# First modulation and block f computed tile by tile of features, with f's weights outside the ring of slots

## The reference

```
mod = einsum(silu(cond), w_ada[l]) + b_ada[l]          # (6 * 1024) per group
sh1, sc1, g1, sh2, sc2, g2 = split(mod, 6)
hn  = rmsnorm(x, norm_mix[l]) * (1.0 + sc1) + sh1
proj = einsum('bld,de->ble', hn, w_in[l])              # q,k,v of attention, retention, HGRN2
...                                                    # three mixers, w_out, gated residual, MoE
```

## Time and profile before

| | us |
|---|---|
| median of 3 runs | 951.66 |
| lowest and highest | 951.46, 954.39 |
| profiled execution: time | 953.32 |
| profiled execution: span | 951.5 |
| TensorE busy in it | 920.2 (97%) |
| VectorE busy | 431.9 (45%) |
| ScalarE busy | 158.7 (17%) |

### The profile page before, as it was taken

How to read it: one execution, slowest core, us unless ns; L and a number is a source line. 1 busy time by engine, 2 the same in 40 slices (tenths; PEclk the granted TensorE clock), 3 DMA queues, 4 the chain that set the end, 5 groups by cost and what they waited for, 6 DMA issues and landing times.

```text
span 951.5 us, 13385 instructions
## 1 busy us (share of the span) xinstructions
PE 920.2 (97%) x5191; PEld 499.6 (53%) x5197; DVE 431.9 (45%) x780; ACT 158.7 (17%) x408; POOL 63.7 (7%) x96
## 2 busy tenths in 40 slices
PE   5999999999999999999999999999999999999997
PEld 2755575568553444344437556657864444443442
DVE  1385887742423122232145999876252321222223
ACT  2212024320210100010111211432021001000100
POOL 1112230020000000000000223000000000000001
PEclk9999999999999999999999999999999999999999
DMA  9996574675999999999996632601189999999993
GB/s 365 401 390 268 222 267 177 243 278 213 408 420 422 421 421 421 421 422 420 421 421 252 225 124 91 235 32 38 35 364 422 421 421 421 421 421 421 421 421 137
DMA packets 48430, 303.63 MB, mean 319 GB/s; under 512 B 7680, under 2 KB 7696, under 8 KB 14960
## 3 DMA queue, kind: packets, MB, share of 16 engines
q1 hardware_dynamic: 42368, 291.52, 75.2%
q0 software_dynamic: 2960, 8.63, 2.6%
q10 hardware_dynamic: 3040, 2.62, 0.8%
HBM read 300.10 MB, written 2.65 MB: 318 GB/s over the span
## 4 chain that ended last, share of the span: by engine, by line
PE 84%; DVE 9%; DMA 3%; ACT 2%; issue 1%; SPq 0%; DVEq 0%; ACTq 0%
PE ps L427 82%; PE ps L461 2%; DMA ring<-in_w_in 2%; ACT eP L1582 1%; DMA ring<-in_w_ada 1%; DVE fa L1263 1%; DVE rt L1057 1%; DVE eP L1361 1%; DVE stat L1057 1%; DVE xy L1257 1%; DVE eP L1359 1%; DVE hnT L1105 0%; DVE sq L1214 0%; DVE proj L1290 0%; DVE proj L1224 0%
## 5 line engine op out<-in xcount | busy, mean ns | idle before, releaser
L427 PE MATMUL ps<-ring,proj 128*64 128x512 f32 x1024 | 226.3, 595 | 1.0 <-ACT proj L1829 1.0
L427 PE MATMUL ps<-ring,hnT 128*128 128x512 f32 (+1 forms) x576 | 203.2, 505 | 2.3 <-issue 1.2
L427 PEld LDWEIGHTS ps<-ring,hnT 128*128 128x128 f32 x576 | 106.9, 191 | 75.9 <-issue 67.7
L427 PEld LDWEIGHTS ps<-ring,proj 128*64 128x64 f32 x1024 | 72.6, 137 | 132.8 <-issue 131.1
L427 PE MATMUL ps<-hnT,ring 128*64 128x128 f32 (+2 forms) x576 | 74.0, 342 | 2.9 <-DVE hnT L1105 1.6
L427 PEld LDWEIGHTS ps<-hnT,ring 128*64 128x64 f32 (+1 forms) x576 | 60.7, 160 | 13.9 <-issue 2.9
L427 PEld LDWEIGHTS ps<-proj,xs 128*128 128x128 f32 x512 | 58.4, 192 | 12.5 <-issue 11.4
L427 PE MATMUL ps<-proj 128*128 128x512 f32 x128 | 61.7, 607 | 0.0
L427 PE MATMUL ps<-proj,xs 128*128 128x128 f32 x512 | 61.4, 278 | 0.1
L1553 DVE COPY proj<-ps 128x512 f32<-128x512 f32 x16 | 11.1, 692 | 108.0 <-PE ps L427 108.0
L427 PE MATMUL ps<-ring,silT 128*32 128x512 f32 x384 | 48.8, 630 | 9.6 <-DVE silT L1073 6.9
(11 more groups left out here) (231 smaller groups left out, 920.9 us busy)
## 6 DMA issues: line engine op xcount, KB each, us to landing
ring<-in_w_gate SPq DMA_DIRECT2D x64, 1024.0 KB, 14.4
ring<-in_w_down SPq DMA_DIRECT2D x64, 1024.0 KB, 16.8
ring<-in_w_ada SPq DMA_DIRECT2D x48, 1024.0 KB, 8.6
ring<-in_w_in SPq DMA_DIRECT2D x28, 1024.0 KB, 8.5
eP<-in_w_up SPq DMA_DIRECT2D x16, 1024.0 KB, 15.8
wT<-in_w_up SPq DMA_DIRECT2D x16, 1024.0 KB, 17.9
fa<-in_w_up SPq DMA_DIRECT2D x16, 1024.0 KB, 17.7
xy<-in_w_up SPq DMA_DIRECT2D x16, 1024.0 KB, 19.1
```

Of the source, the lines that this page charges most:

```text
L427: ins = nc.tensor.matmul(*a, **k)
```

## The change

At the start of layer 0 the adaLN product and block f go by tiles of features.

- The two sixths (0, x) of w_ada are stored a second time, as `ada_x`: eight tiles of 1 MB, each with all rows for one tile of 128 features, shift and scale. One tile alone gives the modulation of its features. TensorE makes of each eight matmuls of 256 columns into four quarters of bank 1 (`sums_of_feature`); ScalarE copies them (256 columns); two matmuls of 2 columns with the new constant `pick` add the quarters and turn them (`modulation_of_feature`); VectorE and ScalarE finish the tile k of hnT; and `feature_of_first_block` adds tile k to all four heads of f at once, in two banks (eight matmuls of 256 columns). The sums of tile k + 1 stand between the picks and the f matmuls of tile k.
- f's two halves are loaded into eP and wT (slots 8 and 9), ahead of adaLN tiles 1 and 4 (`ROWS_AHEAD`). The ring's count begins at two (`FIRST_SLOT`).
- condT, x and the first constants are loaded by SP, ahead of all weights; GpSimd keeps mods. ScalarE starts with group 0 when its x has landed.
- The zeros for TensorE are 14 matmuls, at the very start; they also clear the two banks of f.
- `ADA_BEHIND` of layer 0 goes from (2, 3, 3, 3, 3, 2, 3, 2) to (0, 0, 2, 9, 3, 2, 3, 2): the loads of b stand behind two adaLN slots. The diagonals stand behind block a's last quarter and these two steps; of the nine steps around b, three stand behind each group's first half and three behind b.
- VectorE bounds both heads' pairs first (`bounded(0)`, `bounded(1)`), then makes the gates.

Layer 1 is as before. The diff, cut:

```diff
-ADA_BEHIND = ((2, 3, 3, 3, 3, 2, 3, 2), (0, 0, 0, 0, 0, 3, 0, 0))
+ADA_BEHIND = ((0, 0, 2, 9, 3, 2, 3, 2), (0, 0, 0, 0, 0, 3, 0, 0))
+ROWS_AHEAD = (1, 4)
+FIRST_SLOT = 2
...
                 if l == 0:
-                    for step in EARLY:
-                        load_ada(*step)
+                    for k in range(KC):
+                        if k in ROWS_AHEAD:
+                            r = ROWS_AHEAD.index(k)
+                            load_rows(*IN_BLOCKS[0], r, RING + r)
+                        load(flat_slot, ap["ada_x"][k])
...
+                def sums_of_feature(k):
+                    pe.wait_ge(S("bank1_free"), c.claim(1))
+                    s = slot()
+                    for i in range(KC):
+                        q = slice(32 * (i % 4), 32 * (i % 4) + 32)
+                        last = mm(ps[q, 1, 0:2 * P], silT[:, i, :], ..., start=i < 4, stop=i >= 4)
+                    owed.append(s)
...
+                    f_banks = [next_bank() for _ in range(2)]
+                    pe.wait_ge(c.of("zero", 0), c.at("zero", 0))
+                    stream_zeros(f_banks[0], 12)
+                    stream_zeros(f_banks[1], 2)
+                    normalized_group("hn1", "xn1", 0, banks=(4, 5))
+                    sums_of_feature(0)
+                    normalized_group("hn1", "xn1", 1, banks=(6, 0))
+                    ss = []
+                    for k in range(KC):
+                        modulation_of_feature(k)
+                        if k + 1 in ROWS_AHEAD:
+                            ss.append(slot(RING + len(ss)))
+                        if k + 1 < KC:
+                            sums_of_feature(k + 1)
+                        feature_of_first_block(k, ss, f_banks)
...
                 ss = open_block("b")
+                if not l:
+                    diagonal(0)
+                    diagonal(1)
                 for g in range(NG):
                     b = by_token("b", g, 0, ss)
+                    if not l:
+                        ada_steps(3)
                     level(0, 2 * g)
...
-                ada_behind("b")
+                ada_steps(ADA_BEHIND[l][3] % 6)
                 ss = open_block("i")
...
-                gates(0)
+                bounded(0)
+                if l:
+                    gates(0)
+                    bounded(1)
+                else:
+                    bounded(1)
+                    gates(0)
                 gates(1)
```

More of the change, by code:

```diff
@@ L70, in host_constants @@
     at = [(32 * (2 * a + h), g) for h in range(2) for a in range(2) for g in range(NG)]
+    c["pick"] = np.stack([t % 32 == g for g in range(NG)], 1)
     c["pickm"] = np.stack([t == row + g for row, g in at], 1)
@@ L333, in build @@
         ADA = {"x": (0, 1), "g": (2, 5), "y": (3, 4)}
-        EARLY = [(0, "x", k) for k in range(KC)]
         LATER = [[(0, "g", k) for k in range(KC)] + [(0, "y", k) for k in range(KC)] + [(1, "x", k) for k in range(KC)],
@@ L386, in _ @@
                     for r in range(2):
[L387 to L389 removed]
+                        if l or name != "f":
+                            load_rows(name, col, n, r)
                     for step in itertools.islice(steps, behind):
@@ L482, in claim_for_norm, with normalized_group @@
                 return b
-            def normalized_group(stage, factors, g, ahead=None, first=None):
+            def normalized_group(stage, factors, g, ahead=None, banks=(None, None)):
                 xv = x[:, g].rearrange("p (k q) -> p k q", k=KC)
                 for h in range(2):
-                    b = claim_for_norm() if h or first is None else first
+                    if banks[h] is None:
+                        b = claim_for_norm()
+                    else:
+                        b = banks[h]
+                        pe.wait_ge(S(f"bank{b}_free"), c.claim(b))
                     if not h:
@@ L553, in at_change @@
                         ada_step(*step)
-                if l == 0:
-                    b = claim_for_norm()
-                    for step in EARLY[0:5]:
-                        ada_step(*step)
-                        stream_zeros(b, 3)
-                    pe.wait_ge(c.of("begin_dma"), c.at("begin_dma"))
-                    normalized_group("hn1", "xn1", 0, first=b)
-                    normalized_group("hn1", "xn1", 1)
-                    for step in EARLY[5:]:
-                        ada_step(*step)
-                    modulation_by_feature(0, 0)
-                else:
+                def sums_of_feature(k):
[3 more added lines that the diff above has]
+                        q = slice(32 * (i % 4), 32 * (i % 4) + 32)
+                        last = mm(ps[q, 1, 0:2 * P], silT[:, i, :], by_k(s, 2 * P)[:, i] if i < KH else flat_slot(s)[:, 2 * P * i:2 * P * (i + 1)], start=i < 4, stop=i >= 4)
+                        if i < KC - 1:
+                            pay(last)
+                    last.then_inc(c.fills(1, "ada", 0, "x", k), 1)
+                    owed.append(s)
@@ new lines, in modulation_of_feature @@
+                def modulation_of_feature(k):
+                    pe.wait_ge(S("bank7_free"), c.claim(7))
+                    pe.wait_ge(c.of("modX", 0, 0, k), c.at("modX", 0, 0, k))
+                    for a in range(2):
+                        last = mm(ps[:, 7, NG * a:NG * (a + 1)], modX[:, 2 * P * (k % 2) + P * a:2 * P * (k % 2) + P * (a + 1)], C["pick"], start=True, stop=True)
+                        if not a:
+                            pay(last)
+                    last.then_inc(c.fills(7, "modT", 0, 0, k), 1)
@@ new lines, in feature_of_first_block @@
+                def feature_of_first_block(k, ss, banks):
+                    for g in range(NG):
+                        pe.wait_ge(c.of(f"hn1S{g}", k), c.at(f"hn1S{g}", k))
+                    for p in range(2):
+                        for hl in range(2):
+                            for d in range(2):
+                                col = 64 * (2 * p + hl) + 256 * d
+                                last = mm(ps[64 * d:64 * d + 64, banks[p], 256 * hl:256 * (hl + 1)], by_k(ss[k // KH], 512)[:, k % KH, col:col + 64], hnT[:, k, :], start=False, stop=(k == KC - 1), skip_group_check=True)
+                                if k == KC - 1 and hl and d:
+                                    last.then_inc(c.fills(banks[p], "projP", "f", p), 1)
+                                else:
+                                    pay(last)
@@ L1969, in laid_out @@
     w_out = np.asarray(inputs["w_out"]).reshape(L, D, 2, BLK).transpose(0, 2, 1, 3)
+    first = np.asarray(inputs["w_ada"])[0, :, 0:2 * D].reshape(P, KC, 2, KC, P)
+    out["ada_x"] = first.transpose(3, 0, 1, 2, 4).reshape(KC, P, KC * 2 * P)
     out["w_out"] = halves(w_out, KH).reshape(L, 2, 2, P, KH * BLK)
```

95 lines of the change are left out of this document (53 added, 42 removed).

## The result

The changed kernel takes 962.28 us, median of four runs (960.29 to 963.24), beside 953.02 us of the kernel before on the same chip: ratio 1.0089, 95% interval 1.0063 to 1.0115. It is slower by 0.9%, more than forecast and outside the range. The profiled execution is the fastest of the four: 960.29 us, span 958.5 us, 7.0 us over the 951.5 us of before.

A forecast was written before the change was run, and what follows sets the result against it. TensorE was taken to bound the kernel (84% of the chain). Terms -7.3 (end of f), -1.2 (wait of a), +1.9 (VectorE), +7.9 (slot 1), +1.6 (clock) gave +2.9 us, forecast 954.6 us, range 950.0 to 958.5 us.

The forecast's parts named there:

- T: End of block f: forecast at 41.3 us, 7.3 us earlier than 48.60 us; upper bound 44 us.
- E: End of block b's last quarter, when its slot 1 comes free: forecast at T + 52.5 us.
- some 0.4 us later for the first slot: third at 14.4 us: Start of the weight queue: four small loads ahead on SP delay the first slot 0.4 us; third slot lands at 14.4 us.
- The round: First stage, per feature on TensorE: pick, next feature's sums, f matmuls and changes between them, taken as 3.45 us.
- VectorE: Between T and block i: TensorE waits 0.3 us for hq, 0.6 and 1.0 us for banks; sum 1.9 us, bounds 0 and 4.
- The slot of b: Ahead of i: loads queue behind b's slot 1, released only at E; i at E + 12.5 us, cost 7.9 us.
- The clock: At the start of i: idle stretches bring the clock to half, costing 1.6 us, bounds 0 and 2.5 us.
- Behind i everything is queued as before ... so I take nothing back: After block i: same queue and slots falling together again, so later steps shift by one constant; 0 us.
- slot 1: Ring slot holding part of b; kernel gets over 0.3% faster if its wait costs under 2.2 us with the clock up.
- rival 1: First stage at transfer pace, clock holds: T 38.3 to 40 us, time 950.0 to 951.7 us; chance 0.30.
- rival 2: Clock falls inside the feature loop too, 1.7 us each: 956.3 to 958 us, chance 0.12; low throughout: 973 us, 0.02.
- (3): Ahead of i: slot 1 wait doesn't reach TensorE; i at 98.4 us, -6.5 us, 945.2 us; chance 0.06.

The follow-up runs named there:

- experiment 9: Changed kernel with the small loads (condition, token tiles, constants) issued by GpSimd again, as in the kernel before: 966.7 us, one run.
- Experiment 4: Changed kernel with each feature's f matmuls one round later, behind the next feature's picks and sums: 961.91 us, ratio 1.0083 to the kernel before.
- experiment 10: Changed kernel with the first layer's gates computed ahead of the bounded form again, as in the kernel before: 963.41 us, one run.
- experiment 3: Changed kernel with block b behind five adaLN steps, six left around it: 958.52 us, ratio 1.0041 to the kernel before.
- 12: Changed kernel with b behind eight adaLN steps, seven zero matmuls in the first tile wait, eight more ScalarE copies: 955.2 us, ratio 1.0026.
- experiment 2: Changed kernel with the three waits between b and i filled with matmuls nobody reads: 959.19 us, ratio 1.0042 to the kernel before.
- experiment 7: Changed kernel with 8 more small copies on ScalarE in the first stage: 958.12 us, ratio 1.0051 to the kernel before.
- experiment 1: Changed kernel's new first stage with the old order behind f, so b lies in slots 6 and 7 again: 957.89 us, ratio 1.0049.
- 8: Changed kernel with old order behind f, f matmuls one round later, f's halves ahead of tiles 2 and 6, 8 ScalarE copies: 956.57 us, ratio 1.0029.
- 11: Changed kernel with seven more matmuls of zeros at the entry of the first layer's experts: 963.46 us, one run.
- 13: Changed first stage with old order behind f, plus seven zero matmuls ahead of the second tile's sums and eight ScalarE copies: 957.29 us, ratio 1.0036.
- experiment 5: The kernel before, unchanged, run again for a second profile: 953.67 us.

## Why the prediction was wrong

**The way to i was right in its shape, with three terms off.** Forecast 106.3 us, measured 107.34 us; that it lies so near is partly luck, since an error of +2.6 us (T) and one of -2.0 us (from T to E) cancel.

- T, the end of f: 41.3 forecast, 43.92 measured, near the upper bound of 44. The step that failed first is "some 0.4 us later for the first slot: third at 14.4 us": it came at 15.75 us. The 1.1 MB of x and constants now land first (8.1 us where x lands at 14.7 us in experiment 9), and from 5 to 10 us the engines moved 381 GB/s where they moved 421. The prediction gave the move of these loads to SP a price of 0.4 us and no worth; by experiment 9 it is what makes the first stage shorter. The round measured 3.62 us against 3.45, six times: 1.0 us. The last feature's way took 0.3 us more, with the wait of 1.13 us for ScalarE. Sum 2.6 us. Experiment 4 shows that shorter rounds would not have helped: the tiles pace them then.
- VectorE: 1.9 us of waits forecast, 0.25 us occurred. The waits of 0.6 and 1.0 us for banks at level 0 did not come, while the wait for hq did (0.3 forecast). So E = T + 50.5 instead of T + 52.5. What kept it this small is the order of bounds, by experiment 10. There is no room left here: the chain that ended last is VectorE's from 43.87 us, just ahead of the end of f, to 66.69 us, when hq is ready.
- The slot of b: i at E + 12.9 us, forecast E + 12.5. This step, the clearest of the sum, held, in three pieces of 2.41, 1.41 and 3.09 us. Its measured cost, counted as in the forecast, is 8.3 us (12.9 - 4.64) where 7.9 was forecast. The runs say what I did not ask: whether another order gives the time back. Experiments 3 and 12 only move the wait, from i to b or to both.
- The clock: 1.88 us, forecast 1.6 us, and experiment 2 shows it to be the clock. From 100 to 112 us 5.1 us of clock time were lost; the rest lay in the waits and over the adaLN step between them, where it cost nothing.

With these sizes the sum is -4.7 - 1.2 + 0.25 + 8.3 + 1.9 = +4.5 us where I had +2.9; +4.3 us was measured behind i's first half.

**What made it wrong is the sentence "Behind i everything is queued as before ... so I take nothing back".** This term was put at nothing, and another 2.7 us came there: 1.4 us with out_o_k's issue, shown by experiment 7, 0.5 us in the row behind it (5.38 us for 4.85), 0.7 us in the stretch of the experts, and 0.1 us at the end. A clock fall that before had at 254 us was absent, and it gave nothing: TensorE waited 3.35 us for weights at the change of layers instead, where before waited for none. Why that stretch took 0.7 us more (270.4 us for 269.7) stays open.

**The rest lies between executions.** From profile to profile the forecast was +2.9 us and +7.0 us came: 1.4 us more up to i, 2.7 us behind it. From the forecast of 954.6 us to the median of 962.28 us it is some 7.7 us. Of these 4.1 us are the two just named, and 1.4 us are the base, which was the median of three runs (951.66 us) and is 953.02 us with a fourth. The last 2.3 us come from which executions were profiled: the changed kernel's was the fastest of its four, 2.0 us under its median, while that of before lay 0.3 us over its own. No profile shows these 2.3 us. Over all batches the kernel before had medians of 952.6 to 954.8 us, and single executions from 950.3 to 958.8 us.

**Slips in side sums.** The gain is clear of 0.3% as long as slot 1 costs less than 3.7 us (6.6 - 2.9), not 2.2 us; the lower bound of T with a queue no later than before is 38.7 us (39.1 - 0.4), not 38.3 us, which puts the best case of rival 1 at 950.4 us; the work saved in f is 2.0 us, not 2.1. None of them changes the forecast.

**The rivals.** (1) The first stage at the pace of the transfers: partly so (15.75 us), but they made it later, not earlier. (2) Clock falls in the loop of features: none in the changed kernel's profile; in experiments 1, 8 and 11 there was one between 16 and 22 us, 1.7 us each, in the place that rival 2 names. The case that the Trainium skill describes ("TensorE: Matmul & The Clock Gate", section "HAM oscillation — how this bites in real kernels"), a clock that is down again at every tile, was in none of the traces; the single wait of 3.40 us of experiment 3 brought it down, though, where the picks did not. (3) The slot wait that doesn't reach TensorE: it did.

**Where the gain went.** The first stage did give 4.7 us at T. Three ways to the end of block b were tried, and each waits for weights:

| | end of f | waits for weights behind it | i starts |
|---|---|---|---|
| before | 48.60 | 1.19 | 104.89 |
| changed | 43.92 | 6.91 | 107.34 |
| 3 (b behind five) | 44.43 | 0.82, 3.40 | 103.66 |
| 12 (b behind eight) | 43.75 | 5.42 | 106.09 |
| 1 (old order) | 45.30 | 0.97 | 101.37 |
| 13 (old order, f earlier) | 43.61 | 4.37 | 106.08 |

The one that reached i first, experiment 1, had a later end of f than the changed kernel. No version of the changed kernel that was tried beats the kernel before. Still open is where single executions of one kernel differ. In the changed kernel and in experiment 1 the profiled execution was the fastest (experiment 1: 953.5 us, median 957.9 us), in 3, 8 and 12 it lay 1.7 to 1.9 us over the median. In experiment 1 the executions with a higher mean clock are in the main the shorter ones; in which places the others lose it only a profile of each would tell.

## What to carry to other kernels

When a stage is made shorter, ask first for the place where its successor's weights land, and count the bytes up to there: an earlier end of work that frees no slot and saves no bytes turns into a wait, and each of the waits of 3.4 to 5.4 us here brought TensorE's clock down as well. Weights that share the ring with what is loaded behind them hold up all that stands behind them in the queue, and a wait ahead of their release moves the whole row. "Behind this point all is as before" holds only for the program: the loading of instructions, the clock and a stretch where two bounds lie within 2 us answer to a shift. What the order of first loads is worth, here 5.7 us, has to be asked as well, and not only what it costs.

## What the runs showed of the hardware

- A DMA issue on ScalarE took 0.38 us, or 1.92 to 2.16 us where a packet of ScalarE's instructions was under way (eight traces of each kind); in experiment 7, 8 instructions more ahead of it decided that.
- The clock falls, but for the one at the very end of the kernel, come in portions: 1.7 us lost, twice that, or three times (5.1 us in the changed kernel from 100 to 112 us). The same kernel need not repeat the amount: the kernel before lost 1.7 us around 34 us in its first profile and 3.4 us in experiment 5. The window of that one, where TensorE worked 7.76 of 8 us:

```profile
29.00:37.00 8.00, 7.76 (x57) 6.34 (x59) 3.83 (x18) 3.48 (x10) 0.00 (x0) 0.57 1.01 407
```

- Two loads of 512 KB at the start landed after 3.7 and 5.3 us when they stood ahead of all weights in SP's queue, and after 8.4 and 11.7 us from GpSimd's queue beside them.
